# Loading expert weights in pairs of tiles, with tables laid out by first key

## The reference

```python
def peer(xn, w_query, sub_keys, expert_u, expert_v):
    q = (xf @ w_query).reshape(t, PEER_HEADS, 2, HALF_QUERY)          # 8 heads, two halves of 128
    scores = jnp.einsum('thpk,hpnk->thpn', q, sub_keys)               # 128 keys per half
    v1, i1 = lax.top_k(scores[:, :, 0], PEER_TOPK)                    # 16 of 128
    v2, i2 = lax.top_k(scores[:, :, 1], PEER_TOPK)
    cand = (v1[..., :, None] + v2[..., None, :]).reshape(t, PEER_HEADS, PEER_TOPK * PEER_TOPK)
    best, pos = lax.top_k(cand, PEER_TOPK)
    ...
    experts = (e1 * N_KEYS + e2).reshape(t, PEER_HEADS * PEER_TOPK)   # of 16384 experts
    gates = jax.nn.softmax(best, axis=-1)
    ...
        a = jax.nn.gelu(jnp.einsum('cd,ced->ce', xc, expert_u[ic]), approximate=False) * gc
        return jnp.einsum('ce,ced->cd', a, expert_v[ic])
```

## Time and profile before

| What | Value |
|---|---|
| median of 3 runs | 1619.54 us (1618.03 to 1620.83) |
| profiled execution, its own time | 1618.06 us |
| its span, first to last instruction | 1616.2 us |
| TensorE matmul busy | 1607.6 us, 99% |
| VectorE busy | 1281.6 us, 79% |
| ScalarE busy | 690.6 us, 43% |
| DMA packets, bytes | 126919, 424.34 MB |

### The profile page before, as it was taken

One profiled execution on the slowest core, in us unless ns is written; L12 is line 12 of the kernel. 1 busy time (PEld: TensorE's weight loads), 2 busy tenths in 40 slices (PEclk: granted clock), 3 DMA queues, 4 the chain that ended last, 5 costly groups with the idle time before them and its releaser, 6 DMA issues.

```text
span 1616.2 us, 25174 instructions
## 1 busy us (share of the span) xinstructions
PE 1607.6 (99%) x8581; PEld 1422.9 (88%) x8581; DVE 1281.6 (79%) x2311; ACT 690.6 (43%) x921; POOL 370.1 (23%) x286
## 2 busy tenths in 40 slices
PE   9999999999999999999999999999999999999998
PEld 7888888888888999999999999998888888888887
DVE  6855733335457999998999998778898999998997
ACT  5323423333325433334666766433334333333333
POOL 0000000000000100003222222433453445554551
PEclk9999999999999999999999999999999999999999
DMA  4322332222321655658899999998999999999994
GB/s 170 131 93 97 116 109 91 94 100 94 115 81 64 224 185 194 212 191 334 318 367 364 377 359 374 403 376 324 387 413 367 402 414 398 403 415 393 414 378 161
DMA packets 126919, 424.34 MB, mean 263 GB/s; under 512 B 16384, under 2 KB 19472, under 8 KB 125200
## 3 DMA queue, kind: packets, MB, share of 16 engines
q1 hardware_dynamic: 75168, 232.85, 39.3%
q0 software_dynamic: 39264, 142.64, 23.0%
q10 hardware_dynamic: 12432, 48.26, 7.6%
HBM read 375.18 MB, written 48.51 MB: 262 GB/s over the span
## 4 chain that ended last, share of the span: by engine, by line
PE 99%; DMA 0%; DVE 0%; ACT 0%; SPq 0%; issue 0%; ACTq 0%
PE bank L922 21%; PE bank L923 20%; PE bank L924 20%; PE bank L1104 11%; PE bank L1106 11%; PE bank L1105 11%; PE bank L1082 3%; PE bank L988 1%; DMA w_raw<-w_in 0%; PE bank L968 0%; PE bank L967 0%; PE bank L969 0%; PE bank L1118 0%; DVE u_lo L1203 0%; PE bank L1039 0%; PE bank L940 0%
## 5 line engine op out<-in xcount | busy, mean ns | idle before, releaser
L1157 DVE TENSOR_TENSOR w_lo<-w_raw,w_hi 128x1024 fp32r<-128x1024 f32 x347 | 423.4, 1220 | 147.3 <-ACT w_hi L589 142.3
L589 ACT ACTIVATE w_hi<-w_raw 128x1024 fp32r<-128x1024 f32 x347 | 366.3, 1057 | 353.2 <-PE bank L1106 214.9
L922 PE MATMUL bank<-xn_hi,w_hi 128*128 128x368 f32 (+1 forms) x1472 | 516.6, 351 | 0.1
L924 PE MATMUL bank<-xn_hi,w_lo 128*128 128x368 f32 (+1 forms) x1472 | 510.7, 347 | 0.0
L923 PE MATMUL bank<-xn_lo,w_hi 128*128 128x368 f32 (+1 forms) x1472 | 510.6, 347 | 0.0
L538 POOL DMA_INDIRECT rows<-u_rows,expert x128 | 156.0, 1218 | 958.5 <-DVE expert L1558 544.4
L1104 PE MATMUL bank<-w_hi,a_hi 128*128 128x512 f32 x768 | 298.9, 389 | 0.0
L1106 PE MATMUL bank<-w_hi,a_lo 128*128 128x512 f32 x768 | 298.8, 389 | 0.0
L1105 PE MATMUL bank<-w_lo,a_hi 128*128 128x512 f32 x768 | 298.8, 389 | 0.0
L922 PEld LDWEIGHTS bank<-xn_hi,w_hi 128*128 128x128 f32 x1472 | 276.2, 188 | 17.8 <-issue 0.6
L924 PEld LDWEIGHTS bank<-xn_hi,w_lo 128*128 128x128 f32 x1472 | 276.1, 188 | 17.6
(11 more groups left out here) (225 smaller groups left out, 1381.7 us busy)
## 6 DMA issues: line engine op xcount, KB each, us to landing
w_raw<-u SPq DMA_DIRECT2D x128, 512.0 KB
w_raw<-v SPq DMA_DIRECT2D x128, 512.0 KB
g_dram<-g_sb ACTq DMA_DIRECT2D x12, 2048.0 KB, 10.6
g_in<-g_dram SPq DMA_DIRECT2D x84, 256.0 KB
act_dram<-act_out ACTq DMA_DIRECT2D x54, 384.0 KB
act_in<-act_dram SPq DMA_DIRECT2D x54, 384.0 KB
w_raw<-gate SPq DMA_DIRECT2D x32, 512.0 KB
w_raw<-w_in SPq DMA_DIRECT2D x31, 512.0 KB
```

Source lines behind the costliest of these rows:

```text
L589: act.activation(w_hi[:, slot, :], w_raw[:, slot, :], ACT.Copy).then_inc(hi_done, 1)
L922: pe.matmul(out, hi, x_hi, start=k == 0, stop=False)
L924: last = pe.matmul(out, lo, x_hi, start=False, stop=k == NB - 1)
L1157: dve.tensor_tensor(w_lo[:, slot, :], w_raw[:, slot, :], w_hi[:, slot, :].bitcast(F32), ALU.subtract).then_inc(lo_done, 1)
```

## The change

U and V tiles are loaded two at a time, into slots 0 and 1 or 2 and 3, by one DMA of 1024 KB (`load_pair`); only the first four U tiles still come one by one. The pair's load waits until the slots of both tiles are free, and raises one semaphore, that of the even slot, for which ScalarE waits for either tile (`pairs=True`). In DRAM `u` is now ordered by pairs, so that a partition's two rows lie side by side, 8 KB in one run. `v` and `u_rows` lie as [first key, second key, 1024]: the rows of one e1 for all e2 follow one another, so a V pair reads for each partition e1 two neighbouring rows, again a run of 8 KB. Behind each e1's 128 rows stands one row of zeros (`ROW_STEP` = 129), so that the rows of neighbouring partitions lie 129 x 4 KB = 516 KB apart. The gathers read the same tables, with row number e1 * 129 + e2. In the V stage the even tile's `g_in` piece now stands behind the pair's load.

```diff
--- before.py
+++ after.py
@@ -81,6 +81,7 @@
+ROW_STEP = KEYS + 1
...
@@ -445,6 +446,12 @@
+            def load_pair(source, n, slot):
+
+                sp.wait_ge(lo_done, n + 1 - SLOTS + 1)
+                sp.dma_start(w_raw[:, slot:slot + 2, :].rearrange("p s d -> p (s d)"), source
+                             ).then_inc(raw_loaded[slot], 16)
+
...
@@ -475,19 +482,27 @@
-            load_all(u_d, AT_U, KEYS - N_PIECES)
+            for b in range(SLOTS):
+                sp.wait_ge(lo_done, AT_U + b - SLOTS + 1)
+                sp.dma_start(w_raw[:, b, :], u_d[b // 2, :, b % 2, :]).then_inc(raw_loaded[b], 16)
+            with sp.Fori(1, (KEYS - N_PIECES) // SLOTS) as i:
+                for b in range(0, SLOTS, 2):
+                    load_pair(u_d[ds(SLOTS // 2 * i + b // 2), :, :, :].rearrange("o p s d -> (o p) (s d)"),
+                              SLOTS * i + (AT_U + b), b)
             for k in range(2):
                 sp.wait_ge(g_stored[k], 16 * N_PIECES // 2)
             for piece in range(N_PIECES):
                 e2 = KEYS - N_PIECES + piece
-                load_raw(u_d, e2, AT_U + e2, e2 % SLOTS)
+                if e2 % 2 == 0:
+                    load_pair(u_d[e2 // 2].rearrange("p s d -> p (s d)"), AT_U + e2, e2 % SLOTS)
                 load_g(0, piece)
 
             def load_v_group(g):
 
                 e2 = SLOTS * (g - KEPT_STEPS) % KEYS
                 for b in range(SLOTS):
-                    load_raw(v_d, e2 + b, SLOTS * g + (AT_V + b), b)
+                    if b % 2 == 0:
+                        load_pair(v_d[:, e2 + b:e2 + b + 2, :].rearrange("p s d -> p (s d)"), SLOTS * g + (AT_V + b), b)
                     if b % 2 == 1 and g >= KEPT_STEPS:
 
                         sp.wait_ge(af_ready, b + 1 if g == KEPT_STEPS else SLOTS * (g - 1) + b + 1)
@@ -580,9 +595,9 @@
-            def split_weight(n, slot, times):
-
-                act.wait_ge(raw_loaded[slot], 16 * times)
+            def split_weight(n, slot, times, pairs=False):
+
+                act.wait_ge(raw_loaded[slot - slot % 2 if pairs else slot], 16 * times)
                 if not isinstance(n, int) or n >= SLOTS:
 
                     act.wait_ge(job_done, n - SLOTS + 1)
@@ -744,7 +759,7 @@
-                split_weight(SLOTS * step + (AT_U + SLOTS + b), b, step + (AT_U // SLOTS + 2))
+                split_weight(SLOTS * step + (AT_U + SLOTS + b), b, step + (AT_U // SLOTS + 2), pairs=True)
@@ -853,7 +868,7 @@
-                    split_weight(SLOTS * g + (AT_V + b), b, g + (AT_V // SLOTS + 1))
+                    split_weight(SLOTS * g + (AT_V + b), b, g + (AT_V // SLOTS + 1), pairs=True)
@@ -1555,7 +1570,7 @@
-            dve.scalar_tensor_tensor(expert[:], flat(e2), float(KEYS), flat(e1), ALU.mult, ALU.add
+            dve.scalar_tensor_tensor(expert[:], flat(e1), float(ROW_STEP), flat(e2), ALU.mult, ALU.add
                                      ).then_inc(experts_ready, 1)
...
@@ -1766,6 +1781,11 @@
+def by_first_key(w):
+
+    return np.concatenate([w.reshape(KEYS, KEYS, D), np.zeros((KEYS, ROW_STEP - KEYS, D), np.float32)], 1)
+
+
...
@@ -1793,9 +1813,9 @@
-        "u": a["expert_u"][0].reshape(KEYS, KEYS, NB, P).transpose(1, 3, 2, 0).reshape(KEYS, P, D),
-        "v": a["expert_v"][0].reshape(KEYS, KEYS, D).transpose(1, 0, 2),
-        "u_rows": a["expert_u"][0].reshape(KEYS, KEYS, D).transpose(1, 0, 2),
+        "u": a["expert_u"][0].reshape(KEYS, KEYS // 2, 2, NB, P).transpose(1, 4, 2, 3, 0).reshape(KEYS // 2, P, 2, D),
+        "v": by_first_key(a["expert_v"][0]),
+        "u_rows": by_first_key(a["expert_u"][0]),
```

More of the change, by code:

```diff
@@ L1574, in _ @@
             chain.wait()
-            dve.scalar_tensor_tensor(expert_last[:], e2[:, CHUNKS - 1, :, :].rearrange("p h r -> p (h r)"), float(KEYS),
-                                     e1[:, CHUNKS - 1, :, :].rearrange("p h r -> p (h r)"), ALU.mult, ALU.add
+            dve.scalar_tensor_tensor(expert_last[:], e1[:, CHUNKS - 1, :, :].rearrange("p h r -> p (h r)"), float(ROW_STEP),
+                                     e2[:, CHUNKS - 1, :, :].rearrange("p h r -> p (h r)"), ALU.mult, ALU.add
                                      ).then_inc(last_ready_index, 1)
```

## The result

The changed kernel takes 1641.31 us (median of 4 runs, 1637.54 to 1645.68), the kernel before on the same chip 1619.17 us: ratio 1.0137 [1.011, 1.0164]. It is 22 us slower, and the forecast of 1619.5 us and its range (to 1626) were wrong. The profiled execution took 1642.02 us, with a span of 1640.1.

The account below looks back on a forecast made before the run. The kernel was taken as TensorE-bound from first tile to last: 1616.2 us of span less 0 to 0.1, all other terms 0; with 1.9 us around it and 1.5 to the median, 1619.5 us, range 1617 to 1626.

Parts of the forecast that it names:

- Selection stage: 535 to 700 us: a U pair lands in 6 to 7 us, inside the 7.9 us VectorE allows; cost 0.
- The gathers read as many rows of 4 KB as before: 0: Term for gathers from the reordered tables: same number of 4 KB rows, so no time added.
- V pairs: V stage, 1089 to 1610 us: weights land in 8 to 9 us, inside a 9.9 us margin; cost 0.
- Delay of act_in: V stage: act_in, queued behind the pair, comes 0 to 0.3 us later, 3.5 us at the most; cost 0.
- backlog of 6.5 us: V stage, SP's queue: older bytes ahead at 1307.32 us, worked out from one load, taken to keep act_in from moving.
- Cost: 0: V stage: the price put on the delay of act_in, taken as 0 to 0.3 us.
- 19.4 us of further waiting: V stage spare under rival 1: 11.1 us of free VectorE time plus 8.3 us of lead over TensorE, for 37 act_in loads.
- Rival 1: V stage: late act_in makes VectorE the bound; at 0.75 us more wait per load +9 us, 1628 us; chance 8%.
- Rival 2: Selection stage: a pair lands after more than 7.9 us; +4 us (1624) at 9 us, +14 at 11.0; chance 7%.
- Rival 3: Saturated stages: less DMA time makes the kernel faster, at most −5 us over the V stage, 1614.5 us; chance 5%.
- Rival 4: 8 KB runs get cut into 4 KB packets: packets stay at 126,919, time as forecast; 80% together with the forecast.
- The 40 ns a packet: Estimated fixed DMA cost per packet: 126 pairs save 16,128 packets, 0.65 ms of engine time, 0 in the sum.

Follow-up runs that it names:

- added products: Changed kernel plus 20 products of ones on TensorE ahead of the wait for the last three V tiles; 1634.65 us, 1.0112 against the kernel before.
- one final tile: Kernel before the change with FINAL_TILES = 1, so only the last V tile is held back for the closing order; 1622.16 us, 1.0023.
- act_in first: Changed kernel with act_in issued ahead of the V pair: 1624.56 us, 1.0035; the same with single U tiles: 1621.21 us, 1.0015.
- late halves: Changed kernel, but both tiles of a pair load at the pair's time by two 512 KB DMAs, a semaphore each; 1634.49 us, 1.0098.
- the layouts alone: New layouts and row numbers, but each tile loaded singly when its own slot is free; 1620.42 us, 1.0007 against the kernel before.

## Why the prediction was wrong

**What bounds the kernel: right, and nothing could be gained.** None of the twelve beats it. The layouts, tables and row numbers at 0: right (1.0007).

**Selection stage: right.** U tile 40's pair, issued at 671.76, lands 4.9 us later, under the 6 to 7 I took. ScalarE waits for it, and VectorE's split slips by 1.3 us against the earlier trace rows: just what the whole trace is late by at the first U tiles already (ScalarE's copy at 512.85 before, 514.14 after), where pairs had loaded nothing yet.

```profile
671.76 5.25 SPq L452 DMA_DIRECT2D w_raw<-u  x2
...
676.67 1.06 ACT L604 ACTIVATE w_hi<-w_raw 128x1024 fp32r<-128x1024 f32 x1 [3.66 <-DMA w_raw<-u]
...
680.68 1.22 DVE L1172 TENSOR_TENSOR w_lo<-w_raw,w_hi 128x1024 fp32r<-128x1024 f32 x1
```

**Two tight places: one was missed.** I looked at the selection stage for its busy VectorE and at the V stage for its full DMA engines. At the end of the U stage, from 900 us on, the DMA engines are nearly as full (share 0.96), and I looked at no tile there. SP, then ScalarE:

```profile
1048.85 0.33 SPq L452 DMA_DIRECT2D w_raw<-u  x1
...
1061.00 0.33 SPq L452 DMA_DIRECT2D w_raw<-u  x1
...
1066.70 0.33 SPq L452 DMA_DIRECT2D w_raw<-u  x1
```

```profile
1058.11 1.06 ACT L604 ACTIVATE w_hi<-w_raw 128x1024 fp32r<-128x1024 f32 x1 [4.32 <-DMA w_raw<-u]
...
1069.20 1.06 ACT L604 ACTIVATE w_hi<-w_raw 128x1024 fp32r<-128x1024 f32 x1 [7.64 <-DMA w_raw<-u]
```

Pairs land 9.3 and 8.2 us after issue here. The slots come round every 1066.70 − 1048.85 = 17.9 us, where TensorE wants its four tiles in 16.0. But ScalarE's waits aren't what binds. The chain that ended last, at this place:

```profile
1048.79 9.79 DMA rows<-u_rows,expert
...
1059.83 1.14 DVE w_lo L1172
...
1066.65 10.26 DMA rows<-u_rows,expert
...
1078.16 1.14 DVE w_lo L1172
```

VectorE's program alternates products of gathered rows and splits. It stood for the rows, so the split came late, and SP's pair of 1061.00 went out right behind it; ScalarE's copy for that split was ready at 1053.2. From 1012 to 1085 us the chain runs through four such gathers (13.0, 9.8, 9.8, 10.3 us) and through no load of U. In 900 to 1097 us VectorE waits 22.7 us for rows of u, before 14.1. So a second term failed here: "The gathers read as many rows of 4 KB as before: 0". Why the rows come later wasn't tried, and how much of it is the change's is uncertain. The kernel with added products is the changed one up to 1605 us; there VectorE waits 15.9 us, TensorE never waits at this place, and the V stage begins at 1090.5. With single U loads it begins at 1087.8 to 1091.2 in six profiles (five of the table, and 1090.9 in before with one final tile, whose U stage is that of the kernel before), with U tiles loaded at the pair's time at 1090.5 to 1096.1 in eight. Pairs for U alone cost 0.24%.

**V pairs: right that they cost nothing themselves.** ScalarE waits 32.2 us for them, and with act_in first such waits are free. (For w_raw in all I had forecast 10 to 60 us; with U's 72.1 it is 104.3.)

**The step that failed: "Delay of act_in: 0 by that, 3.5 us at the most; I take 0 to 0.3".** It rested on "While SP's queue is backlogged by more than 3.5 us, a later arrival of half the bytes ahead doesn't move act_in". The bytes ahead are the same with late halves, and act_in waits went from 6.4 to 25.5 us. So the backlog of 6.5 us that I worked out from one load, with half of the 405 GB/s taken for SP's queue without a row, doesn't shield act_in. I had also taken act_in to be issued when it was, and left out that the even tile's g_in piece now stands right ahead of it. In size the step was off by little: the waits grow by 20.9 us over 54 loads from before to after, at least 0.4 us a load.

**With it failed "Cost: 0" behind it.** At my own 0.3 us a load the waits would have grown by 16 us, and the table shows that this isn't free: late halves, with 15.5 us more than before, have a V stage 6.1 us longer. The spare was overrated. I had 19.4 us of further waiting; the edge near 20 lies only some 9 us above before's 11.0. That is about TensorE's lead of 8.3; of the 11.1 us in which VectorE seemed free in 300, the runs show none that could be had. I had also set the spare against the 37 loads of that stretch, where the lead has to last for the whole stage.

**Rival 1 is what happened.** I gave it 8%. Its price, +9, lacked three things: that smaller spare, the sum over all loads, and the close, where TensorE waits for three tiles together (5.9 us) and then runs at half clock (2 us). Late act_in is therefore 15.9 of the 23.9 us between the two spans: with act_in first those 15.9 are gone. The other 8.0 are the slow clock at the start (1.3), ScalarE's long issue (2.9) and the end of the U stage (3.7).

**Rival 2** didn't happen: in the selection stage the pair landed in time, and at 1050 us, where pairs kept ScalarE waiting, the chain runs through the gathers. **Rival 3** fell. **Rival 4** fell: packets did get fewer, by 126 × 144, not 126 × 128, since each DMA left out also takes 16 small packets along. The 40 ns a packet, 0.65 ms for the pairs, didn't come out: by the shares of its page SP's queue took 10.13 ms of engine time after and 10.16 before (10.41 with the layouts alone).

**Open.** Why gathered rows of u land late at the end of the U stage, and whether pairs are the reason: U pairs and V pairs together begin the V stage at 1094.3 to 1096.1 in five profiles, but at 1090.5 in the one with added products. How much of act_in's delay is the weights' later moment and how much the g_in piece ahead of it. How far the 8 KB runs hold up gathers between them.

## What to carry to other kernels

Loading two buffers by one DMA halves the number of DMAs and makes each slot's turn longer: in a ring of four, follow one tile, and the gathers beside it, in every stage in which the DMA engines are full, not only in the one with the busiest engine. When a load grows, price what stands behind it in its queue: here the weights could wait 32 us for nothing, and the 384 KB behind them could not. Idle time of an engine is no spare until a run shows that it can be had. Its lead over the engine that it feeds is a spare, but only once for the whole stage. So sum the small waits to the stage's end, and ask what the program does when the last tile comes late.

## What the runs showed of the hardware

- TensorE standing for 5.9 us (6.8 us with pairs in V alone) is followed by some ten matmuls of 512 columns at 0.43 us, the pace of 1.2 GHz; after 1.8 us, following small products, there is none (0.23 us from the second one on).
- ScalarE can stand at the issue of a DMA: that of an act_dram store at 933 to 935 us took 5.71 us before and 9.17 after, with no other work of ScalarE meanwhile; TensorE stood 2.4 us behind it after, and not at all before. The longest issue is 5.7 to 8.5 us in the six kernels with single U loads, and 9.2 to 10.5 us in the eight with U tiles loaded at the pair's time. The cause of it wasn't tried.
- A load of 384 KB behind 1 MB, at 376 to 405 GB/s over all queues, lands 10.4 us after issue on average before and 10.8 after, where VectorE waited for it, at most 11.4 and 12.8.
